# Scan stage: a second step order on TensorE and VectorE, all additions of the output on VectorE

## What is computed

```python
decay = jnp.exp(jnp.where(lower, seg, -jnp.inf))
cb = jnp.einsum('bctgn,bcsgn->bctsg', cc, bc)
y_diag = jnp.einsum('bctsgh,bcsghp->bctghp', cb[..., None] * decay, xdt)
states = jnp.einsum('bcsgn,bcsghp->bcghpn', bc, xdt * decay_end[..., None])
h_last, h_in = lax.scan(step, h0, (states, chunk_decay))    # step: h * dec + st
y_off = jnp.einsum('bctgn,bcghpn->bctghp', cc, h_in) * jnp.exp(a_cs)[..., None]
y = y_diag + y_off
...
y = (y_f + _flip_seq(y_r) + xh.astype(f32) * d_skip...)
```

## Time and profile before

| | |
|---|---|
| median of 3 executions | 1669.87 us (1667.97 to 1678.6) |
| the profiled execution, its own time | 1665.68 us |
| its span, first to last instruction | 1663.6 us |
| mean granted TensorE clock | 0.885 |
| busy: TensorE, VectorE, ScalarE, GpSimd | 1380.5, 835.2, 669.0, 271.2 us |
| scan loop | about 729 to 979 us of the span |

### The profile page before, as it was taken

How to read it: one execution, slowest core, us unless ns; L and a number is a source line. 1 busy time by engine, 2 the same in 40 slices (tenths; PEclk the granted TensorE clock), 3 DMA queues, 4 the chain that set the end, 5 groups by cost and what they waited for, 6 DMA issues and landing times. The chain is left out here.

```text
span 1663.6 us, 20622 instructions
## 1 busy us (share of the span) xinstructions
PE 1380.5 (83%) x7925; PEld 1200.5 (72%) x7925; DVE 835.2 (50%) x959; ACT 669.0 (40%) x1028; POOL 271.2 (16%) x278
## 2 busy tenths in 40 slices
PE   3999989899989999567678854999984489999980
PEld 1799989799988889335456743998873378888860
DVE  2412432476661111273454549333346089999966
ACT  3433220244441221335445637111022077777753
POOL 0600000000000100245656732000004100000002
PEclk9999999899999999796777756999976799999985
DMA  9972211122113431632333432322534589999945
GB/s 387 406 291 76 77 51 54 58 77 76 65 52 118 138 124 42 202 92 98 114 102 122 164 128 82 116 96 73 200 151 168 203 314 411 406 413 409 415 175 202
DMA packets 61639, 289.09 MB, mean 174 GB/s; under 512 B 8171, under 2 KB 12787, under 8 KB 41206
## 3 DMA queue, kind: packets, MB, share of 16 engines
q1 hardware_dynamic: 48566, 242.18, 38.9%
q0 software_dynamic: 12608, 45.62, 7.0%
q10 hardware_dynamic: 384, 0.16, 0.0%
HBM read 239.51 MB, written 48.43 MB: 173 GB/s over the span
## 5 line engine op out<-in xcount | busy, mean ns | idle before, releaser
L212 PE MATMUL banks<-rounded,rounded 128*128 128x320 f32 (+1 forms) x1168 | 365.5, 313 | 19.9 <-DVE rounded L735 6.6
L213 PE MATMUL banks<-rounded,rounded 128*128 128x320 f32 (+1 forms) x1168 | 363.4, 311 | 0.0
L214 PE MATMUL banks<-rounded,rounded 128*128 128x320 f32 (+1 forms) x1168 | 363.3, 311 | 0.0
L212 PEld LDWEIGHTS banks<-rounded,rounded 128*128 128x128 f32 (+1 forms) x1168 | 220.6, 189 | 21.2 <-issue 13.9
L191 DVE TENSOR_TENSOR rounded<-words,rounded 128x2048 fp32r<-128x2048 f32 x52 | 119.2, 2292 | 226.0 <-ACT rounded L183 223.7
L1877 DVE TENSOR_TENSOR rounded<-words,rounded 128x2048 fp32r<-128x2048 f32 x93 | 212.9, 2290 | 34.1 <-ACT rounded L1868 33.2
L213 PEld LDWEIGHTS banks<-rounded,rounded 128*128 128x128 f32 (+1 forms) x1168 | 220.7, 189 | 0.4
L214 PEld LDWEIGHTS banks<-rounded,rounded 128*128 128x128 f32 (+1 forms) x1168 | 220.5, 189 | 0.3
L1868 ACT ACTIVATE rounded<-words 128x2048 fp32r<-128x2048 f32 x96 | 183.7, 1916 | 48.2 <-PE banks L1995 40.0
L183 ACT ACTIVATE rounded<-words 128x2048 fp32r<-128x2048 f32 x52 | 99.2, 1908 | 138.0 <-PE banks L233 61.2
L1169 ACT ACTIVATE words<-words,words 128x128 f32<-128x128 f32 x320 | 97.8, 388 | 125.5 <-DMA words<-decay_sums 125.5
(11 more groups left out here) (270 smaller groups left out, 2058.4 us busy)
## 6 DMA issues: line engine op xcount, KB each, us to landing
words<-in_units SPq DMA_DIRECT2D x52, 1024.0 KB, 5.0
words<-in_wg SPq DMA_DIRECT2D x32, 1024.0 KB, 7.6
words<-in_wu SPq DMA_DIRECT2D x32, 1024.0 KB, 7.7
words<-in_wd SPq DMA_DIRECT2D x32, 1024.0 KB, 8.5
words<-decay_sums SPq DMA_DIRECT2D x40, 512.0 KB, 3.8
words<-in_w_mod_rest SPq DMA_DIRECT2D x32, 512.0 KB, 5.6
slot_rows<-words POOLq DMA_DIRECT2D x27, 512.0 KB, 24.3
expert_rows<-words POOLq DMA_DIRECT2D x25, 512.0 KB, 9.5
```

The costliest lines, as they stand in the source:

```text
L212: nc.tensor.matmul(out, lhs[0](k), rhs[0](k), start=(k == 0), stop=False)
L213: nc.tensor.matmul(out, lhs[0](k), rhs[1](k), start=False, stop=False)
L214: last = nc.tensor.matmul(out, lhs[1](k), rhs[0](k), start=False, stop=(k == nk - 1))
```

## The change

TensorE computes the state parts of step j+1 ahead of the diagonal product of step j, and does state product, parts and modulation behind the diagonal product. VectorE evacuates the product of step j-1 ahead of scaling the state parts of step j, and makes three additions for it instead of one: the two state parts, diagonal plus skip, and their sum. `finish_y` is gone from GpSimd, which only multiplies; it scales rows two steps ahead instead of one (XT has three buffers), and weighs last. The carry of a state moves to the odd step. SO lies where OF is, and GpSimd waits once for its stores.

```diff
-    XT = kit.at(O_HL + 6144, 4, 256)
-    SO = kit.at(O_HL + 7168, 2, 512)
+    XT = kit.at(O_HL + 6144, 6, 256)
+    SO = kit.at(O_TMP + 1792, 2, 512)
...
             def time_rows(j):
-                if j >= 2:
-                    pool.wait_ge(y_done, j - 1)
+                if j >= 3:
+                    pool.wait_ge(y_done, j - 2)
...
-            def finish_y(j):
-                pool.wait_ge(off_scaled, j + 1)
-                pool.wait_ge(skip_ready, j + 1)
-                nc.gpsimd.tensor_tensor(OF[:, j % 2, 1, :], YK[:, j % 2, :], OF[:, j % 2, 1, :], ALU.add).then_inc(rest_ready, 1)
-                pool.wait_ge(y_steps, j + 1)
-                pool.wait_ge(rest_ready, j + 1)
-                nc.gpsimd.tensor_tensor(X[:, c, ...], V1[:, j % 2, :], OF[:, j % 2, 1, :], ALU.add).then_inc(y_whole, 1)
...
+            for j in range(2):
+                pool.wait_ge(state_stored[j], 16 * NX // 2)
             for j, (c, g, q) in enumerate(subs):
-                if j in x_at:
-                    weigh(pool, nc.gpsimd, x_at[j])
-                if j >= NL + 2:
+                if j >= 2:
                     pool.wait_ge(y_steps, j - 1)
                 (the skip term, unchanged)
-                if 1 <= j < NL + 1:
-                    finish_y(j - 1)
-                if 1 <= j < NS - 1:
-                    time_rows(j + 1)
+                if j + 2 < NS:
+                    time_rows(j + 2)
+                if j in x_at:
+                    weigh(pool, nc.gpsimd, x_at[j])
```

```diff
         TensorE
+            def off(j):
+                c, g, q = subs[j]
+                if not c:
+                    return
+                if j >= 2:
+                    pe.wait_ge(off_scaled, j - 1)
+                elif j == 0:
+                    pe.wait_ge(states_loaded, 48)
+                    pe.wait_ge(state_carried, NF - NX)
+                if c < 4:
+                    pe.wait_ge(state_carried, NF - NX + 4 * (3 - c) + g + 1)
+                (the two products of the state parts)
             prepare(0)
+            off(0)
             for j, (c, g, q) in enumerate(subs):
                 if j + 1 < NS:
                     prepare(j + 1)
-                if j in x_at:
-                    state(x_at[j])
-                if j in at_sub:
-                    add_parts(at_sub[j] - 1)
-                    modulate(at_sub[j])
+                    off(j + 1)
                 if j >= 2:
                     pe.wait_ge(y_steps, j - 1)
-                (the two products of the state parts, with their waits)
                 (the diagonal product)
+                if j in x_at:
+                    state(x_at[j])
+                if j in at_sub:
+                    add_parts(at_sub[j] - 1)
+                    modulate(at_sub[j])
         VectorE
             def scale_off(j):
-                if j >= 2:
-                    dve.wait_ge(y_whole, j - 1)
                 dve.wait_ge(off_done, j + 1)
...
             def take_y(j):
-                dve.wait_ge(y_done, j + 1)
                 if c:
                     dve.wait_ge(off_scaled, j + 1)
-                    nc.vector.tensor_tensor(V1[:, j % 2, :], v, OF[:, j % 2, 0, :], ALU.add).then_inc(y_steps, 1)
+                    nc.vector.tensor_tensor(OF[:, j % 2, 0, :], OF[:, j % 2, 0, :], OF[:, j % 2, 1, :], ALU.add).then_inc(rest_ready, 1)
+                dve.wait_ge(y_done, j + 1)
+                dve.wait_ge(skip_ready, j + 1)
+                last = nc.vector.tensor_tensor(V1[:, j % 2, :] if c else rows, v, YK[:, j % 2, :], ALU.add)
+                last.then_inc(y_steps, 1)
+                if c:
+                    dve.wait_ge(rest_ready, j + 1)
+                    dve.wait_ge(y_steps, j + 1)
+                    nc.vector.tensor_tensor(rows, V1[:, j % 2, :], OF[:, j % 2, 0, :], ALU.add).then_inc(y_whole, 1)
...
+                if j:
+                    take_y(j - 1)
                 if c:
                     scale_off(j)
-                if j:
-                    take_y(j - 1)
                 if j in at_sub:
                     take_part(at_sub[j])
-                if j in x_at:
-                    x = x_at[j]
+                if j - 1 in x_at:
+                    x = x_at[j - 1]
                     dve.wait_ge(state_carried, x - NX - 3)
                     carry(x)
```

More of the change, by code:

```diff
@@ L1106, in _ @@
             pe.wait_ge(sums_taken, 1)
+            def off(j):
[9 more added lines that the diff above has]
+                    pe.wait_ge(state_carried, NF - NX + 4 * (3 - c) + g + 1)
+                ct = CT[:, g, c * P:(c + 1) * P]
+                w4 = slice(g * GW + q * 256, g * GW + (q + 1) * 256)
+                nc.tensor.matmul(ps[:, 5 + j % 2, 0:256], ct, hF[:, c - 1, w4], start=True, stop=True)
+                nc.tensor.matmul(ps[:, 5 + j % 2, 256:512], ct, hb(c)[:, w4], start=True, stop=True).then_inc(off_done, 1)
             prepare(0)
+            off(0)
             for j, (c, g, q) in enumerate(subs):
@@ L1132, in _ @@
                         at = d * 512 + h * P
-                        last = nc.tensor.matmul(o, E[:, j % SLOTS, at:at + P], XT[:, 2 * (j % 2) + d, h * HD:(h + 1) * HD],
+                        last = nc.tensor.matmul(o, E[:, j % SLOTS, at:at + P], XT[:, 2 * (j % 3) + d, h * HD:(h + 1) * HD],
                                                 start=(d == 0), stop=(d == 1))
                 last.then_inc(y_done, 1)
+                if j in x_at:
[3 more added lines that the diff above has]
+                    modulate(at_sub[j])
             add_parts(NP - 1)
@@ L1239, in take_y @@
                 c, g, q = subs[j]
[L1240 to L1241 removed]
                 if c:
                     dve.wait_ge(off_scaled, j + 1)
[L1244 to L1248 removed]
+                    nc.vector.tensor_tensor(OF[:, j % 2, 0, :], OF[:, j % 2, 0, :], OF[:, j % 2, 1, :], ALU.add).then_inc(rest_ready, 1)
+                dve.wait_ge(y_done, j + 1)
+                dve.wait_ge(skip_ready, j + 1)
+                v = ps[:, 2 + j % 2, 0:256]
+                rows = X[:, c, g * GW + q * 256:g * GW + (q + 1) * 256]
+                last = nc.vector.tensor_tensor(V1[:, j % 2, :] if c else rows, v, YK[:, j % 2, :], ALU.add)
[4 more added lines that the diff above has]
+                    nc.vector.tensor_tensor(rows, V1[:, j % 2, :], OF[:, j % 2, 0, :], ALU.add).then_inc(y_whole, 1)
             def masks(gi):
```

19 lines of the change are left out of this document (1 added, 18 removed).

## The result

The changed kernel takes 1658.21 us (median of 14 executions, 1651.18 to 1667.38), the kernel before 1671.04 beside it (14, 1663.3 to 1683.2). The ratio is 0.9925, 95% interval 0.9898 to 0.9951: faster by 0.75%, 12.8 us, where 28 were forecast. The sign was right and the time lies in the stated range, but the gain is too small for "faster by over 1%".

The account below looks back on a forecast made before the run. The prediction took A as a loop of waits, the last part of B as bound by GpSimd, C by TensorE. Changes of -40.3, +1.8 and +11.3 sum to -27.2 us: 1638.5, with 4.2 to the median 1642; range 1620 to 1664.

Parts of the forecast that it names:

- faster by over 1%: Whole kernel: the outcome under 1653 us, given a chance of 0.82.
- the loop that goes: In A, VectorE waits 93.9 us for state products and GpSimd 74.1 for VectorE's evacuation; the change breaks it.
- the loop that comes: In A, a remaining loop between VectorE and TensorE, with 10.8 us a pair at full clock.
- C: Scan loop from step 32 to the end: 44.9 us against 33.6, +11.3, at the lower clock.
- the serial loop: In B, matrix, diagonal, masks, parts, modulation and copies follow one another on VectorE and TensorE: 9.1 us a pair.
- B: Scan loop steps 20 to 32: 63.8 us against 62.0, +1.8.
- I take nine pairs at full clock and one at the lower: TensorE's clock in A: nine pairs of 10.8 us and one of 14.6, 111.8 in all.
- A: Scan loop steps 0 to 20: 111.8 us against 152.1, -40.3.
- low throughout: Rival for TensorE's clock in the whole scan loop: always low, kernel slower by 31.0 us, giving 1701; chance 0.08.
- a clock above 0.85: Sign for A in the profile after: granted TensorE clock above 0.85, with A at 108 to 116 us.
- the terms for the adds: VectorE's additions in the odd step: 0.41 us each, 1.10 for three operations, plus 0.3 a pair waiting for GpSimd.
- rival 3: VectorE's four adds of a pair each wait 0.5 us for GpSimd: 32 us in sixteen pairs, giving 1674; chance 0.10.

Follow-up runs that it names:

- mods_ahead: Changed kernel with adding parts and the modulation put ahead of the diagonal product on TensorE; ratio to the kernel before 0.9706.
- filler: Changed kernel with one unused 256-column product more per step, ahead of TensorE's wait for the matrix; ratio to the kernel before 0.9868.
- adds_on_pool: Changed kernel with the two final additions back on GpSimd and VectorE's single evacuation; ratio to the kernel before 0.9986.
- mods_skip_filler: mods_skip with one unused 256-column product more per step, ahead of TensorE's wait for the matrix; ratio to the kernel before 0.9651.
- mods_skip: Changed kernel with parts and modulation ahead of the diagonal and GpSimd's skip term released by VectorE's last addition; 1607.35 us, ratio to the kernel before 0.9605.
- skip_later: Changed kernel with GpSimd's skip term released by VectorE's last addition instead of by the evacuation; ratio to the kernel before 0.9898.

## Why the prediction was right and wrong

**Right: the loop that goes, and the loop that comes.** The wait of 93.9 us for the state parts is gone, and TensorE waits for the matrix as forecast. A pair at the full clock takes 11.1 us, forecast 10.8, and TensorE's two waits in it are 1.54 and 0.94 us, forecast 1.6 and 1.0.

**Right: C and the serial loop.** C is 43.9 us against 44.9 (the last step, taken at 4.75, waits for no new matrix and takes 3.4). In its timeline a step with masks starts 5.99 us after the last (931.88 to 937.87) and one with a modulation 7.33 (937.87 to 945.20); the terms were 1.31 + 3.44 + 1.27 = 6.02 and 1.31 + 3.44 + 2.44 = 7.19:

```profile
931.88 3.65 PE L1127 MATMUL banks<-words 128*128 128x64 f32 x16 [1.64 <-DVE words L1264]
935.32 0.74 PE L1056 MATMUL banks<-words 128*128 128x128 f32 x2
937.87 3.65 PE L1127 MATMUL banks<-words 128*128 128x64 f32 x16 [1.82 <-DVE words L1264]
941.45 0.58 PE L1075 MATMUL banks<-words,words 128*2 128x128 f32 x2
...
945.20 1.08 PE L1127 MATMUL banks<-words 128*128 128x64 f32 x4 [1.64 <-DVE words L1264]
```

mods_ahead confirms the cause. **B** is 65.6 against 63.8; its fastest pair is 9.1, exactly the sum given for it, and its first pairs 12.7 and 11.2 against 11.5 each.

**Wrong, and the failed step: "I take nine pairs at full clock and one at the lower".** Four of ten pairs were at the full clock, and the lower one cost 13.2 us of A instead of 3.8, that is 9.4 of the 12.4 us missing. The forecast took a pair as all full or all low, at 14.6. No pair was all low: in the timeline above, a pair of 14.3 still has one of its two diagonal products at 1.97. The low clock came in parts, spread over six pairs at 1.5 to 3.2 us each, and added up to what 3.5 low pairs of the forecast cost. filler, which leaves all dependencies as they are, takes 11.1 us off A. The waits were read rightly; what failed is the step from them to the clock. The argument was B's busy share (22.5 of 27.2 us) against 8.2 of 10.8 in the new pair, one row of a busier stretch taken for the rule, while C, busier than both, stood at 0.50 in the earlier trace rows. The rival "low throughout" had 0.08; nothing between it and the forecast had a price, and the own range of the forecast was two or three pairs of ten. Why the clock falls in some of these equal pairs and not in others stays open. The sign "a clock above 0.85" came true at 0.87 and so was too loose to tell.

**Wrong: the terms for the adds.** They were taken at 0.41, with 0.69 as the upper bound, plus 0.3 a pair for contention. L1249 takes 0.87. The path in the odd step, from L1239's start to L1231's (772.89 to 774.54), is 1.65 instead of 1.10; with the 0.3 it is 0.25 too little, and a pair 11.1 instead of 10.8: 3 us in A. The exclusion was read correctly in the earlier trace rows, and rival 3 was right about the mechanism. What was missed is that it is no chance meeting: the skip term and the add have the same releaser, L1244. Rival 3's other reason against, that GpSimd is idle for most of a pair, says nothing when both start together. Its price was half of a GpSimd operation for four adds; it is 0.45 us for L1249 in each step and 0.84 more for L1239 in the even one, 1.7 a pair where four times 0.5 was taken, so the delay was priced well; but only the odd step's 0.45 is on the path.

**The whole.** 9.4 + 3.0 us in A, 1.8 in B, less 1.0 in C: 13.2 us, with which the forecast sum of -27.2 becomes the loop's -14.0 in the profiled execution. The median is 16.2 us above the forecast. Of these 12.7 are this execution's (1651.18 against 1638.5). Another 2.8 come from the step to the median: the forecast added 4.2, and the change's median lies 7.0 above its profiled execution. The last 0.7 is rounding in the prediction, whose own sum gives 1642.7 and not 1642.

**What the prediction took as one change is three.** It credited all of A to all three edits. The parts alone show that swapping two calls on VectorE is enough for 1.45%, that TensorE's order alone gives 0.65% after its loss in C, and that moving the additions gains 0.6% where both new orders stand. With TensorE's order of before it was tried only together with the carry's move and others, and lost 1.5%.

## What to carry to other kernels

Two operations on VectorE and GpSimd that both read two SBUF tiles, released by the same event, collided here in 32 steps of 32, however idle GpSimd was; release the one that nobody waits for by the other's end. Price a clock that can fall between its two levels with a range over how often it falls, and compare edits by pairs or steps at one level: the lower clock took 13.2 us of A here, as much as the whole change gained, and in adds_on_pool it hid that the pair itself was shorter. And take an edit in several parts apart before judging it: the best version (0.9605) keeps the change, puts three lines back and moves one wait, and the swap of two calls alone (0.9855) did at least as well as the whole change (0.9925).

## What the runs showed of the hardware

- In C TensorE was busy for 32.3 of 32.8 us (mods_ahead) with products of 64 columns, and the granted clock stayed at 0.50. With a product of 256 columns more in each step it was 0.50 in filler and 0.55 in mods_skip_filler, while the same product brought it from 0.87 to 0.97 in A (change to filler) and from 0.81 to 0.97 in B (mods_skip to mods_skip_filler), and left the A of the kernel before at 0.70, from 0.72. What sets it in C was not found.
- The exclusion chains: the row scaling L1006 (1.54 us instead of the 1.04 it has at 781.67) held the matrix L1264 (1.34 instead of 1.21), which held the weighing L937 (2.02 instead of 1.04), which held L1239 (1.26 instead of 0.42). The Trainium skill (SBUF — State Buffer, section Who interferes with whom) has a VectorE instruction with at most one SBUF input, outside the two-port modes, free of it. The trace agrees: L1195 and L1231, which read PSUM and one SBUF tile, began under a running L1006 ten and eight times and took their 0.69 and 0.68 us each time. The evacuation L1244, of the same kind, says nothing on it: none of its 40 ran beside a GpSimd operation.
- The clock's falls are no property of the code alone: skip_later's pairs in A, all of one code, ran from 10.7 to 15.2 us, and the change's 14 executions spread over 16 us.
